# Four of the sixteen gate products of layer 2 moved from VectorE to GpSimd

## The reference

```
a, ag, z = split(h @ w_in_c, 3)
glu = a * sigmoid(ag)
y = causal_depthwise_conv(ext(glu), w_conv_c) + b_conv_c     # 31 taps
y = silu(layer_norm(y, ln_c_g, ln_c_b))
out = (y * silu(z)) @ w_out_c
```

## Time and profile before

| | us |
|---|---|
| median of three runs | 2132.11 |
| the profiled execution | 2129.69 |
| its span, slowest core (core 7) | 2128.1 |
| spans of the eight cores | 2120.0 to 2128.1 |
| TensorE busy | 2058.0 (97%) |
| VectorE busy | 1061.8 (50%) |
| ScalarE busy | 678.7 (32%) |
| GpSimd busy | 346.9 (16%), nearly all of it issuing DMAs |

### The profile page before, as it was taken

One profiled execution on the slowest core, in us unless ns is written; L12 is line 12 of the kernel. 1 busy time (PEld: TensorE's weight loads), 2 busy tenths in 40 slices (PEclk: granted clock), 3 DMA queues, 4 the chain that ended last, 5 costly groups with the idle time before them and its releaser, 6 DMA issues.

```text
span 2128.1 us, 38961 instructions; the slowest of 8 cores (2120.0 to 2128.1 us)
## 1 busy us (share of the span) xinstructions
PE 2058.0 (97%) x15797; PEld 1287.7 (61%) x15797; DVE 1061.8 (50%) x1520; ACT 678.7 (32%) x894; POOL 346.9 (16%) x669
## 2 busy tenths in 40 slices
PE   3999999999999999999999999999999999999997
PEld 1645666466666666666666665566665666666664
DVE  3545250652554544655555322656334757747646
ACT  3255303643011112111120344651445622222341
POOL 1001101010011100011000654013552000100100
PEclk9999999999999999999999999999999999999998
DMA  9945646086376664477653997576987643633734
GB/s 206 161 112 94 106 79 109 11 131 108 58 109 97 100 104 76 69 119 106 105 82 69 199 192 160 105 139 126 205 193 152 121 91 67 119 70 70 147 57 161
DMA packets 92993, 244.03 MB, mean 115 GB/s; under 512 B 17040, under 2 KB 40976, under 8 KB 92560
## 3 DMA queue, kind: packets, MB, share of 16 engines
q0 software_dynamic: 57040, 192.60, 52.9%
q1 hardware_dynamic: 35232, 48.28, 8.3%
q10 hardware_dynamic: 544, 0.66, 0.1%
HBM read 344.92 MB, written 13.76 MB: 169 GB/s over the span
## 4 chain that ended last, share of the span: by engine, by line
PE 90%; DMA 3%; ACT 3%; DVE 2%; issue 2%; POOL 0%; SPq 0%; DVEq 0%; ACTq 0%; POOLq 0%
PE ps L501 76%; PE ps L852 4%; PE ps L619 3%; PE ps L1253 3%; DMA ring<-w_ada 1%; PE ps L1133 1%; ACT ysT L1336 1%; DMA ring<-w_in_a 1%; PE ps L989 1%; PE ps L395 1%; DMA xa_sb<-xa 1%; DMA tmp<-tmp 0%; PE ps L451 0%; PE ps L1287 0%; DVE ysT L1343 0%
## 5 line engine op out<-in xcount | busy, mean ns | idle before, releaser
L501 PE MATMUL ps<-hT,ring 128*128 128x352 bf16 (+1 forms) x8448 | 1288.2, 313 | 10.5 <-ACT tmp L1299 2.3
L501 PEld LDWEIGHTS ps<-hT,ring 128*128 128x128 bf16 x8448 | 821.0, 98 | 469.6 <-issue 29.3
L501 PE MATMUL ps<-ysT,ring 128*128 128x352 bf16 (+1 forms) x2688 | 410.6, 313 | 8.7 <-DVE xb_sb L590 4.3
L501 PEld LDWEIGHTS ps<-ysT,ring 128*128 128x128 bf16 x2688 | 260.2, 97 | 158.7 <-issue 15.8
L162 POOL DMA_DIRECT2D tmp<-tmp x320 | 161.5, 560 | 102.0 <-PE ps L1287 55.6
L1205 DVE TENSOR_TENSOR tmp<-tmp,ps 128x1074 bf16<-128x1074 f32 (+3 forms) x64 | 45.5, 711 | 168.8 <-PE ps L501 162.3
L852 PE MATMUL ps<-ring,hT 128*128 128x512 bf16 x544 | 120.3, 379 | 1.6 <-DMA ring<-w_in_a 0.8
L1079 DVE TENSOR_TENSOR tmp<-tmp,ps 128x1074 f32<-128x1074 f32 (+3 forms) x64 | 45.4, 710 | 142.8 <-PE ps L501 132.2
L1068 ACT ACTIVATE tmp<-ps 128x1074 f32<-128x1074 f32 (+1 forms) x32 | 33.9, 1059 | 252.8 <-PE ps L501 252.8
L1261 ACT ACTIVATE tmp<-ps,cst_sb 128x16 bf16<-128x16 f32 (+2 forms) x160 | 69.8, 437 | 132.5 <-PE ps L1253 120.6
L584 DVE SCALAR_TENSOR_TENSOR xa_sb<-ps,modT,xa_sb 128x1074 f32<-128x1074 f32 (+1 forms) x32 | 42.5, 1327 | 116.0 <-PE ps L501 115.9
(11 more groups left out here) (196 smaller groups left out, 1706.4 us busy)
## 6 DMA issues: line engine op xcount, KB each, us to landing
ring<-w_in_b POOLq DMA_DIRECT2D x64, 512.0 KB, 6.8
ring<-w_ada POOLq DMA_DIRECT2D x48, 512.0 KB, 6.4
ring<-w_in_a POOLq DMA_DIRECT2D x48, 512.0 KB, 11.0
ring<-w_in_c POOLq DMA_DIRECT2D x48, 512.0 KB, 7.3
ring<-w_in_d POOLq DMA_DIRECT2D x24, 512.0 KB, 6.3
tmp<-tmp POOLq DMA_DIRECT2D x160, 69.4 KB, 4.4
tmp<-tmp POOLq DMA_DIRECT2D x160, 67.5 KB, 4.7
ysT<-tmp SPq DMA_DIRECT2D x64, 132.0 KB, 4.8
```

The source lines that it names most:

```text
L501: ins = h.matmul(PSB[:, 3 * sl + n, 0:W], lhsT=lw, rhs=rh[:, n * W:(n + 1) * W], start=(first and k == 0), stop=(last and k == len(pairs) ...
```

## The change

`product(c)` is recorded for GpSimd instead of VectorE where c is 2, 5, 8 or 11; operands, output and place in the recorded order are the same. It happens once per group, so eight products move.

```
         def product(c):
             y = ysT[:, c, 0:NC]
             z = ZS[c % 6]
-            s.op("dve", lambda h: h.tensor_tensor(out=y, in0=y, in1=tb(z, NC), op=ALU.mult), reads=["ys.%d" % c] + tk(z, 537), writes=["ys.%d" % c])
+            s.op("pool" if 2 <= c < 13 and c % 3 == 2 else "dve", lambda h: h.tensor_tensor(out=y, in0=y, in1=tb(z, NC), op=ALU.mult), reads=["ys.%d" % c] + tk(z, 537), writes=["ys.%d" % c])
```

## The result

The changed kernel took 2148.31 us (median of 5 runs), the kernel before 2132.11; the ratio is 1.0086 with a 95% interval of 1.0073 to 1.0099, so about 18 us slower (16 to 21). By 2% that is the same, as forecast; in direction and size it is the loss of the prediction (2149).

What follows compares the result with a forecast made beforehand. TensorE was taken as the bound, busy 2058.0 of 2128.1 us. Product 8's stall net of savings, +15.0 us over both groups, plus 2 x 2.1 for product 11's hold-off made +19, stated as 2149 us; range 2139 to 2161.

Steps and rivals of the forecast that it cites:

- What bounds: Layer 2's tail: TensorE bounds the kernel; a shorter VectorE chain can give at most about 0.5 us per group.
- Products 2 and 5: Early in the tail, where TensorE leads: GpSimd is free when their SiLU ends, and moving them costs nothing.
- The length P: Duration of one product on GpSimd: 0.55 + 1056 x 1.5 ns = 2.15 us, from the memset slope.
- The other estimate: Product duration on GpSimd from the Trainium skill's 2.6 cycles per element: 2.3 us, making the sum about 1 us higher.
- Product 8: GpSimd's queue: stands behind a load awaiting the second w_fold write; SiLU of z 14 8.2 us late, group 0 +7.1.
- Who waits: Behind SiLU of z 14: SiLU of tile 10, centre of tile 13, first output tile's slot; TensorE stalls 5.9 us.
- Product 11: In VectorE's chain at the tail's end: GpSimd's product holds VectorE off for its length, +2.1 us per group.
- Starving: Rival (0.08): back-to-back VectorE instructions keep winning over GpSimd, delaying products 2 and 11; +10 us more, 2159.
- The clock: TensorE after its stall may run at 1.2 GHz: put at nothing, up to 2 us per group if it lasts.
- The sum: Both groups: 2 x 2.1 + 15.0 = +19 us on the profiled 2129.7 us; 2149 stated.

Runs made afterwards that it cites:

- product 8 with its stall gone: Changed kernel with the two ring slots that w_fold is written from released behind product 8 in GpSimd's queue; against the kernel before 1.0015, +3 us.
- the run with product 7: Only product 7 on GpSimd, all other products on VectorE, against the kernel before: ratio 1.0106 (1.0046 to 1.0166), +23 us.
- product 8 alone: Only product 8 on GpSimd, the other fifteen products on VectorE, against the kernel before: ratio 1.0077, +16 us.
- one instruction (0.13 us here): All products on VectorE, a two-column GpSimd memset in product 8's queue place, against the kernel before: ratio 1.0060, +13 us.

## Why the prediction was right

- **What bounds.** Right. Taking products 2 and 5 off VectorE gave nothing (1.0001), and product 8 with its stall gone changed nothing either: 1.0015 with it and without it.
- **Products 2 and 5.** Right that they cost nothing, with one row misread: GpSimd was not free at 1362.1. In the trace before, a ring load (L140) runs from 1361.88 to 1362.41, and product 2 stands behind it. SiLU of z of tile 8 still waits no longer than before, 0.28 us against 0.26.
- **The length P.** Forecast 2.15 us; 2.19 where VectorE stands, and 1.96 in the run with product 7. That was luck: the memset slope hit it although it was one input against two, and was itself not general: 1408 bf16 columns took 1.27 us, 0.9 ns a column. The other estimate, 2.3 us, would have added 0.15 us to two products in each of two groups, 0.6 us and not about 1.
- **Product 8.** Forecast behind the load that waits for the second w_fold write; there it is, on the record of the DMA, and the release moved behind it takes 15 of 18 us away. Forecast 8.2 us late for SiLU of z 14 from core 7. On core 2 it moved from 1391.93 to 1401.25, 9.0 us without the 0.28 of offset; there the second write took 11.1 us to land, against 10.4 in the row that the forecast used.
- **Who waits.** As forecast: SiLU of tile 10, the centre of tile 13, the first output tile's slot. TensorE stood 6.75 us, forecast 5.9.
- **Product 11.** Forecast that VectorE is held off for 2.1 us, 1.5 net; one L1328 takes 3.00 instead of 1.26 us, so 1.74, and 1.1 net. With it the wide instruction shows the direction that the earlier trace rows did not: VectorE, back to back, held by GpSimd. The Trainium skill (SBUF — State Buffer, section Who interferes with whom) is borne out in both directions. At product 2 GpSimd ends 1.81 us behind the VectorE instruction it waited for (1365.68 against 1362.62 + 1.25), and VectorE's next ends 1.11 us behind GpSimd (1366.79); at product 11 the same two differences are 1.81 and 1.11 us.
- **Starving.** The rival's mechanism exists at product 5: 4.52 us. When its record starts, at 1373.55, VectorE's L1334 of 1372.62 has 0.32 us left; two more VectorE instructions are let ahead after it. It cost nothing, because product 5 has 6 us to spare. It did not come at product 11.
- **The clock.** Put at nothing, with up to 2 us per group in the range. The 84 matmuls took 15.34 us against 12.78, at a granted 0.50 and later 0.90 on average; this row of after has PEclk behind the five engines:

```profile
1402.45:1405.00 2.55, 2.55 (x9) 1.28 (x10) 1.13 (x1) 2.55 (x3) 0.00 (x0) 0.50 0.99 135
```

  These 2.56 us are hidden: TensorE still waits 0.59 us for product 15. With product 8 alone there is nothing left to hide them, since the two chains end level. The parts add up within their intervals: 16 for product 8 and 3 for the rest make 19, against 18 (16 to 21) measured.
- **The sum.** +19 forecast from the profiled execution; 9.55 + 9.48 = 19.0 in the trace. By group the forecast was 7.1 + 2.1 = 9.2 and 7.9 + 2.1 = 10.0. The mechanism was right; that the sums agree to the microsecond is partly luck, since the stall of group 0 was 0.8 us longer than forecast and the hold-off 0.4 us shorter in each group.

No kernel that was run beats the one before. With the stall gone, product 11 holds VectorE off for 1.75 us where it saves 0.62; products 2 and 5 save nothing, and product 5 does not hold VectorE off.

## What to carry to other kernels

An engine that looks idle may be standing in a queue: before work is given to it, read what its queue holds around that place and what each of those instructions waits for, and ask who waits for the work in turn. A price found for one instruction (0.13 us here) says nothing of what its place costs (13 us for two of them). Where a load or store shares a queue with arithmetic, record the arithmetic ahead of the transfer whose wait is long.

## What the runs showed of the hardware

A wide two-input GpSimd instruction and a VectorE instruction with two SBUF inputs took turns whole: 3.00 us instead of 1.25 on VectorE in every case where GpSimd was let in between two of its instructions. In the changed kernel GpSimd was let in at products 2 and 11 behind the one instruction in flight when its record started, at product 5 only behind that one and two more, in both groups; its record started 0.24 us ahead of the first of these two. A GpSimd memset of 1408 bf16 columns beside such VectorE instructions (1.25 us each) held nothing off.
